# Dense quarters between the small products of the scan's input stage, and the second transposes in banks 0 and 1

## What is computed

```python
proj = rms_norm(x, g_mix) @ w_in                        # q, k, v, u and two gates
q = rms_norm(q.reshape(b, t, N_HEADS, HEAD_DIM), g_q)   # the same for k
...
# S5 branch: u in groups of 16 channels, complex diagonal state of 64 per group
bu_re = jnp.einsum('btgc,gpc->btgp', ug, bb_re)
bu_im = jnp.einsum('btgc,gpc->btgp', ug, bb_im)
_, _, hr, hi = lax.associative_scan(combine, (ar_full, ai_full, bu_re, bu_im), axis=1)
y = jnp.einsum('btgp,gcp->btgc', hr, c_re) - jnp.einsum('btgp,gcp->btgc', hi, c_im)
```

## Time and profile before

| what | us |
|---|---|
| median of three runs | 1073.25 (1070.86 to 1073.57) |
| profiled execution | 1070.31 |
| its span | 1068.6 |
| TensorE busy | 997.7 (93%) |
| DVE busy | 574.7 (54%) |
| ACT busy | 367.3 (34%) |
| mean granted TensorE clock | 0.982 of full speed |

### The profile page before, as it was taken

The page is one execution under the profiler, slowest core; times in us unless marked ns, Lnnn a source line. Parts: engine busy times, 40 slices in busy tenths (PEclk is TensorE's granted clock), DMA queues, the critical chain, the costliest instruction groups (busy, mean ns, idle before and its releaser), DMA issues.

```text
span 1068.6 us, 17629 instructions
## 1 busy us (share of the span) xinstructions
PE 997.7 (93%) x7694; PEld 952.2 (89%) x7694; DVE 574.7 (54%) x720; ACT 367.3 (34%) x499; POOL 57.7 (5%) x107
## 2 busy tenths in 40 slices
PE   2899888999899999989899999999999999998896
PEld 1798878997888888889899999999999999998896
DVE  2569739941344542437466455555555555569552
ACT  3443222333545454353333222222222222224531
POOL 5000002220100013010000000000000000000000
PEclk9999898999999999999999999999999999999999
DMA  9332212471341118532223322222232222222202
GB/s 202 67 83 59 65 46 76 123 139 44 90 155 62 45 62 307 191 129 80 59 80 88 100 80 79 80 79 80 81 91 86 79 82 92 85 90 62 60 12 78
DMA packets 134413, 97.48 MB, mean 91 GB/s; under 512 B 19681, under 2 KB 124321, under 8 KB 134305
## 3 DMA queue, kind: packets, MB, share of 16 engines
q1 hardware_dynamic: 128192, 79.88, 26.0%
q0 software_dynamic: 5104, 16.47, 5.2%
q10 hardware_dynamic: 1040, 0.00, 0.1%
HBM read 86.36 MB, written 9.85 MB: 90 GB/s over the span
## 4 chain that ended last, share of the span: by engine, by line
PE 80%; DVE 9%; ACT 5%; issue 3%; POOL 2%; DMA 1%; ACTq 0%; POOLq 0%; DVEq 0%
PE dense L1675 67%; PE banks L1675 4%; PE scoreA L1675 3%; PE scoreB L1675 3%; PE banks L1760 2%; DVE tm L1238 1%; DVE wlo L1262 1%; ACT whi L959 1%; DVE mt L1238 1%; DVE R L1238 1%; DVE mt L1297 0%; DMA sm<-gates_spill 0%; DVE dtmp L1328 0%; ACT xsq L1047 0%; DVE gnat L1238 0%
## 5 line engine op out<-in xcount | busy, mean ns | idle before, releaser
L1675 PE MATMUL dense<-act_hi,whi 128*128 128x288 f32 x1152 | 254.2, 303 | 0.8 <-ACT vT L1000 0.8
L1675 PE MATMUL dense<-act_hi,wlo 128*128 128x288 f32 x1152 | 249.0, 299 | 0.0
L1675 PE MATMUL dense<-act_lo,whi 128*128 128x288 f32 x1152 | 248.5, 298 | 0.0
L1262 DVE TENSOR_TENSOR wlo<-wraw,whi 128x1024 fp32r<-128x1024 f32 x126 | 154.2, 1224 | 79.7 <-ACT whi L959 78.5
L1675 PEld LDWEIGHTS dense<-act_hi,whi 128*128 128x128 f32 x1152 | 186.8, 192 | 6.5 <-issue 5.9
L1675 PEld LDWEIGHTS dense<-act_hi,wlo 128*128 128x128 f32 x1152 | 187.1, 191 | 0.0
L1675 PEld LDWEIGHTS dense<-act_lo,whi 128*128 128x128 f32 x1152 | 186.2, 190 | 0.0
L1675 PE MATMUL dense<-hid,whi 128*128 128x288 f32 x1024 | 178.6, 297 | 2.7 <-DVE dtmp L1328 2.7
L959 ACT CAST whi<-wraw 128x1024 fp32r<-128x1024 f32 x126 | 132.2, 1050 | 90.6 <-PE dense L1675 90.5
L1675 PEld LDWEIGHTS dense<-hid,whi 128*128 128x128 f32 x1024 | 150.3, 188 | 3.0 <-DVE wlo L1262 3.0
L1675 PE MATMUL dense<-hid,wlo 128*128 128x288 f32 x512 | 110.1, 296 | 0.0
(11 more groups left out here) (309 smaller groups left out, 1137.7 us busy)
## 6 DMA issues: line engine op xcount, KB each, us to landing
wraw<-in_w_in SPq DMA_DIRECT2D x32, 512.0 KB, 4.1
wraw<-in_w_up SPq DMA_DIRECT2D x32, 512.0 KB, 4.0
wraw<-in_w_down SPq DMA_DIRECT2D x32, 512.0 KB, 3.4
gates_spill<-gst POOLq DMA_DIRECT2D x16, 288.0 KB, 2.5
page<-in_cache_k SPq DMA_DIRECT2D x16, 256.0 KB, 3.4
page<-in_cache_v SPq DMA_DIRECT2D x16, 256.0 KB, 6.6
wraw<-in_w_out SPq DMA_DIRECT2D x8, 512.0 KB, 4.1
wraw<-in_w_ple_gate SPq DMA_DIRECT2D x8, 512.0 KB, 3.9
```

Of the source, the lines that this page charges most:

```text
L1262: return nc.vector.tensor_tensor(out=lo, in0=whole, in1=f32(hi), op=ALU.subtract)
L1675: return nc.tensor.matmul(out, lhsT, rhs, start=start, stop=stop, skip_group_check=True)
```

## The change

The helper `ut` is gone. Each of the four groups is now: `ut`, the first `qknorm` pair, a quarter of a dense unit (blocks 0 and 1, or 4 and 5), the second pair, `ug`, and another quarter. So unit 11 is spread over the first two groups and unit 12 over the last two. `begin` remembers how far a unit has been begun, so that it can be called several times. `ug` has its places in banks 0 and 1 instead of 2 and 3. Everything before `ut` of the first group and from the s products on stands as it was. The line numbers of the engines' code are four higher in the changed kernel.

```diff
@@ -124,10 +124,13 @@
                 dense_job(("m", n[0], j))
             n[0] += 1
 
+    begun = {}
+
     def begin(k1):
 
         flush()
-        event("part", n[0], 0, k1)
+        event("part", n[0], begun.get(n[0], 0), k1)
+        begun[n[0]] = k1
 
     def half_unit():
 
@@ -190,24 +193,25 @@
         event("gt", 1, i, place=2 + i % 2)
     event("qkrstd")
 
-    def ut(q, *ps):
+    def qknorm(p):
         for half in range(2):
-            event("ut", q, half, place=half)
-        for p in ps:
-            for half in range(2):
-                event("qknorm", p, half, place=2 + half)
-        for half in range(2):
-            event("ug", q, half, place=2 + half)
+            event("qknorm", p, half, place=2 + half)
 
     unit()
     event("s5c", 1)
     unit()
-    ut(0, 0, 1)
-    unit()
-    ut(1, 2, 3)
-    ut(2, 4, 5)
-    unit()
-    ut(3, 6, 7)
+    for q in range(4):
+        for half in range(2):
+            event("ut", q, half, place=half)
+        qknorm(2 * q)
+        begin(4 * (q % 2) + 2)
+        qknorm(2 * q + 1)
+        for half in range(2):
+            event("ug", q, half, place=half)
+        if q % 2:
+            unit()
+        else:
+            begin(4)
     for i in range(4):
         for part in range(2):
             event("s", i, part, place=2 * (i % 2) + part)
```

## The result

Four runs of the changed kernel gave a median of 1057.68 us (1056.22 to 1062.97), four of the kernel before 1072.72 us: a ratio of 0.987, 95% interval 0.984 to 0.990, about 15 us where 8.8 were forecast, and below the range given. Two later comparisons of the same two kernels gave 1061.38 against 1071.98 us (ratio 0.990, 0.988 to 0.991) and 1060.47 against 1070.99 (0.991, 0.988 to 0.994). The last of the three ran on another chip than the one before it and gave nearly the same ratio. All together, 14 runs of the changed kernel have a median of 1060.97 us and 45 of the kernel before 1071.98: **11.0 us**. The two later medians lie within the range of the prediction (1060.3 to 1068.5), the first does not. So two things have to be explained: what the stage gave, and why the first comparison showed 4 us more than all of them together.

The account below looks back on a forecast made before the run. TensorE, 80% of the chain, was taken to bound the kernel through waits and low clock. Gaps −5.75, unit 12's clock −1.52 and the s products' −1.73 sum to −9.0, taken as −8.8: 1063.6 us, range 1060.3 to 1068.5.

Parts of the forecast that it names:

- Steps 1 to 3: In the four groups, quarters and changed banks remove TensorE's waits: small products 18.67 to 12.9 us with switching, −5.75 us.
- step 5: Switching between small and dense work in the groups: 0.1 us per group, 0.4 us added, range 0 to 0.7.
- Step 3's margin of 0.43 us: Before the next uT transposes and the s products, DVE finishes its UT copies 0.43 us before TensorE arrives.
- Step 4: Weight splits queued on ACT and DVE between qknorm pairs delay nothing: costed at zero, at most 2.4 us.
- Step 6: Shorter pieces without dense work keep the stage's clock at 1.00: unit 12 −1.52 us, s products −1.73 us.
- The rival of the falling clock: Quarters bring the clock to 0.50 throughout the stage, making the kernel slower: some 1078 us, chance 0.05.
- Survival behind the stage: DVE's scan starts 0.25 us later relative to unit 13; products waiting for it have 4.9 us slack, gain survives.
- The range: Whole-kernel time 1060.3 to 1068.5 us, allowing for switching, one low-clock stretch more or less, and a 2.7 us run spread.

Follow-up runs that it names:

- half units between: Changed kernel with whole groups, second transposes in banks 2 and 3, and half a dense unit behind each group: 1066.28 us, ratio 0.994 to the kernel before.
- the banks alone: Kernel before, old order, with only the second transposes moved to banks 0 and 1: 1066.40 us, ratio 0.996 to the kernel before.
- the quarters with the old banks: Changed kernel with its quarters kept but the second transposes back in banks 2 and 3: 1067.02 us, ratio 0.995 to the kernel before.
- half units inside: Changed kernel with half a dense unit between each group's two qknorm pairs and nothing between groups: 1067.54 us, ratio 0.995 to the kernel before.

## Why the prediction was wrong in its number, and which of its steps held

**Steps 1 to 3, the gaps.** Right. Forecast 12.5 + 0.4 us for the small products and 12.98 for the dense ones, 25.9 us up to s; measured 150.54 − 125.07 = 25.47. Two terms were off and cancel in part, the small products by −1.1 us and the dense ones with their switching by +0.65. The small products are cheaper than I took them: a pair is 126.72 − 126.03 = 0.69 us (I had read the row's length, 0.75, which overlaps the next start), and the second transposes 0.53 (I had taken the old 0.67, which held a wait for their second half). A quarter inside a group costs 128.52 − 126.72 = 1.80 us and one between groups 131.41 − 129.73 = 1.68 (1.78 before s), where a quarter of a unit was to be 1.62: the switching of step 5 is about 0.18 × 4 + 0.06 × 3 + 0.16 = 1.06 us, above my upper bound of 0.7. That bound came from a misread row: 6.61 us is the row's length of unit 13, which overlaps the next start, while 6.49 for unit 11 is from start to start. From start to start unit 13 is 170.62 − 164.12 = 6.50 us, so the rows held no upper bound at all.

**Step 3's margin of 0.43 us.** Held everywhere; without the second quarter it is a wait of 0.83 to 1.30 us, as measured.

**Step 4.** Right: DVE waits 0.23 us between the split and the second pair.

**Step 6, the clock.** Right in size: no low stretch in the stage in any of three traces, s at 4.15 us (4.05 forecast), dense quarters at full pace. Its reason was too narrow. I tied the fall to the double group and to the 0.91 us wait; half units between whole groups show one behind a single group. What the traces show is this: the four with undivided groups (the kernel before twice, the banks alone, half units between) all have a low stretch in the stage, and the five with a quarter or a half inside each group (the change three times, the quarters with the old banks, half units inside) have none. Which property of an undivided group (3.56 busy of 4.43 us, all small products) brings the clock down behind one and not behind the next, they don't show.

**The rival of the falling clock.** Didn't happen in three executions. The Trainium skill's rule ("TensorE: Matmul & The Clock Gate", "A second HAM failure mode: psum-queue depth-cycling") that short idles between groups of matmuls make the clock swing agrees with the kernel before, with the banks alone and with the half units between, where the undivided groups have such idles. The trace doesn't agree with it where dense work stands inside the groups: the quarters with the old banks idle 0.69 us four times and the half units inside 0.83 us three times, and the clock stays at 1.00 in both. In the changed stage there are no idles, so it doesn't apply.

**Survival behind the stage.** Right: the last scan level ends at 213.65 + 2.49 = 216.14 and the products that wait for it start at 221.05, 4.9 us later, as before. The first scores start at 260.98 instead of 269.28 us, 8.3 us earlier where the stage gave 9.3; the difference is the low clock between unit 13 and the scores in this trace.

```profile
213.65 2.49 DVE L1242 TENSOR_TENSOR Hb<-Hb,sc 128x992 f32<-128x992 f32 x3
```

```profile
221.05 0.60 PE L1679 MATMUL banks<-Tm,UT 128*72 128x128 f32 x4
```

**The range.** This is the step that failed. I wrote that "one low stretch more or less elsewhere" and "the spread of the runs of 2.7 us" bound what isn't the stage, and centred the forecast on 8.8 us less than the runs of one kernel. What isn't the stage varies by far more, and almost only by the clock. The stage itself gave 9.3 us where the sum had 9.0; had the first comparison come out like either of the other two, the number would have stood, so that part of the miss is luck. Five executions of the two kernels, worked out from starts in their timelines and from their spans:

| execution | up to the stage | stage | unit 13 to first scores | from there to the end | unit 13 to the last matmul | of it at the low clock |
|---|---|---|---|---|---|---|
| before, first | 125.17 | 38.95 | 105.16 | 799.3 | 898.4 | 20.5 |
| before, second | 123.61 | 38.95 | 105.16 | 801.5 | 900.6 | 25.0 |
| changed, first | 125.07 | 29.62 | 106.29 | 793.5 | 893.8 | 10.2 |
| changed, second | 125.04 | 29.63 | 109.17 | 800.0 | 903.1 | 32.0 |
| changed, third | 122.52 | 29.63 | 103.53 | 802.1 | 899.7 | 23.9 |

Only the stage differs between the kernels by more than it does between executions of one. The last two columns, which end at the start of the last matmul, show why: from the changed kernel's first trace on, each microsecond more at the low clock adds some 0.42 to 0.46 us, in both kernels, near the 0.45 that the prediction worked out for unit 12. The traces of the banks alone (893.9 us with 10.2 low), of the quarters with the old banks (902.6, 32.0), of the half units between (903.0, 32.0) and inside (900.8, 28.5) lie within 0.8 us of the line with 0.42. So behind the stage nothing but the clock differs by more than a microsecond.

The first trace of the changed kernel had the shortest end, 793.5 us, and so its profiled time, 1056.22, is 14.1 us below the profiled time of before: 9.3 from the stage, 5.8 from the end, less 1.1 from the stretch before the scores. Some 3 of those 5.8 us stand at the value transposes, and the rest at two low stretches of 3.4 us that the kernel before has at 271.6 and 991.8 us and this trace lacks. At the value transposes TensorE waits 1.29 and 0.67 us for ACT in all five traces. Kernel before, the stretch with those waits and the next two:

```profile
288.70:292.10 3.40, 1.44 (x10) 1.00 0.82 259
292.10:295.50 3.40, 3.40 (x13) 0.50 0.97 308
295.50:298.90 3.40, 3.40 (x13) 0.50 0.81 248
```

The changed kernel's first trace, the same place:

```profile
278.80:282.20 3.40, 1.44 (x11) 1.00 0.82 257
282.20:285.60 3.40, 3.40 (x22) 1.00 0.94 294
```

And its second:

```profile
281.70:285.10 3.40, 1.45 (x11) 0.99 0.82 257
285.10:288.50 3.40, 3.40 (x13) 0.50 1.00 325
288.50:291.90 3.40, 3.40 (x14) 0.50 0.76 237
```

TensorE is busy 1.44 or 1.45 of 3.4 us in all three. Behind it the clock is at 0.50 for 6.8 us in the first and the third and stays at 1.00 in the second (the other two executions of the table have 6.8 us too, so the changed kernel's first is the exception): 13 records where 22 stood, and over the 134.4 us from the first scores on a mean of 0.96, 1.00 and 0.97. The same kernel falls there in one execution and not in the next.

Two things stay open. All comparisons together give 11.0 us, the stage 9.3. The 1.7 us between them may be chance (the changed kernel's 14 runs spread from 1056.0 to 1065.5) or a later part that falls less often in one kernel than in another; the banks alone, 5.6 us faster with 0.2 us less of stage, and the half units between, 5.7 us with 2.3, speak for the second, though with one trace each their stages may be shorter in other executions. And the runs of the kernel before spread less, 43 of 45 within 1067 to 1074; that fits its low stretches standing at the same places in both traces, but why they repeat there and not in the changed kernel isn't shown.

## What to carry to other kernels

Where small products hand their banks to another engine in turn, put between two users of the same bank as much independent dense work as that engine's reading takes; it has to be at both hand-overs, and a change of banks and a change of order can be worth much less apart than together. A stretch of small products with waits can cost twice, in itself and in the clock that the work behind it gets. And before a gain of a few microseconds is forecast, add up what the low clock costs in each part of the trace: what one execution has there, the next may not, so the range has to hold it. To compare two traces, take the low stretches off both first: here that left 1 us of difference in 900.

## What the runs showed of the hardware that wasn't expected

The granted clock falls behind the same wait in one execution and not in the other, and a low stretch lasts 3.4 us in one and 6.8 us in the other, with the same instructions: 103.5 to 109.2 us for the same 859 records. The part before the stage varies in the same way, from 122.5 to 125.2 us. A change from dense to small products and back costs next to nothing where the small ones are transposes (a quarter of 1.68 us), but 0.18 us where they are norm products (1.80 us). And the waits alone don't bring the clock down: with dense work inside the groups it stayed at 1.00 through waits of 0.69 and 0.83 us, and behind undivided groups it fell somewhere in the stage in every trace.
